# Decode attention over paged keys: both pages of a step in one score block, their rotary rows in one product and one transpose

## What is computed

```python
ckv_past = cache_ckv[page_table].reshape(b, past, KV_RANK)    # 16 pages of 128 positions x 256, per sequence
kr_past  = cache_krope[page_table].reshape(b, past, QK_ROPE)  # 128 positions x 64
sc = (einsum('bqhr,bkr->bhqk', q_lat, ckv) + einsum('bqhe,bke->bhqk', q_rope, k_rope)) * SOFTMAX_SCALE
p = softmax(sc); o_lat = einsum('bhqk,bkr->bqhr', p, ckv)
```

## Time and profile before

| | us |
|---|---|
| median of 3 runs | 518.49 |
| lowest, highest | 518.28, 519.22 |
| the profiled execution: its time | 518.8 |
| its span from first to last instruction | 517.0 |
| PE busy in the span | 501.8 |
| VectorE, ScalarE, GpSimd busy | 349.6, 287.0, 82.8 |

### The profile page before, as it was taken

The page is one execution under the profiler, slowest core; times in us unless marked ns, Lnnn a source line. Parts: engine busy times, 40 slices in busy tenths (PEclk is TensorE's granted clock), DMA queues, the critical chain, the costliest instruction groups (busy, mean ns, idle before and its releaser), DMA issues.

```text
span 517.0 us, 12185 instructions
## 1 busy us (share of the span) xinstructions
PE 501.8 (97%) x4738; PEld 443.0 (86%) x4738; DVE 349.6 (68%) x656; ACT 287.0 (56%) x588; POOL 82.8 (16%) x100
## 2 busy tenths in 40 slices
PE   8999999999999999999999999999999999999993
PEld 7999999899999999899999755666676699999992
DVE  4843668694657666653433468699987899997753
ACT  6543312206357275653624865689996879663631
POOL 1321000000001000000000142235554303100710
PEclk9999999999999999999999999999999999999997
DMA  8642112249798888979986152945625577879722
GB/s 260 242 163 83 63 61 103 88 133 344 242 316 301 285 298 278 335 255 312 295 299 215 46 136 39 232 120 118 153 74 210 203 248 217 287 238 334 258 90 82
DMA packets 58075, 104.15 MB, mean 201 GB/s; under 512 B 7465, under 2 KB 27346, under 8 KB 57890
## 3 DMA queue, kind: packets, MB, share of 16 engines
q1 hardware_dynamic: 58018, 103.37, 62.2%
HBM read 95.68 MB, written 7.76 MB: 200 GB/s over the span
## 4 chain that ended last, share of the span: by engine, by line
PE 81%; DVE 6%; ACT 5%; DMA 4%; issue 2%; POOL 0%; SPq 0%; DVEq 0%; ACTq 0%
PE pm L1632 17%; PE pm L1634 16%; PE pm L1633 16%; PE px L1728 4%; PE px L1748 3%; PE pm L1929 3%; PE pm L1859 3%; PE px L1910 2%; PE pm L1897 2%; DMA dec<-ac_dram 2%; DVE w_lo L992 2%; DMA w_raw<-in_w_out 1%; PE px L1850 1%; PE px L1873 1%; PE pm L1921 1%
## 5 line engine op out<-in xcount | busy, mean ns | idle before, releaser
L1632 PE MATMUL pm<-xw_hi,w_lo 128*128 128x260 f32 x544 | 158.0, 290 | 0.4 <-DVE xw_lo L1125 0.4
L1633 PE MATMUL pm<-xw_lo,w_hi 128*128 128x260 f32 x544 | 153.7, 283 | 0.0
L1634 PE MATMUL pm<-xw_hi,w_hi 128*128 128x260 f32 x544 | 153.6, 282 | 0.0
L595 ACT ACTIVATE w_hi<-w_raw 128x1024 fp32r<-128x1024 f32 (+1 forms) x70 | 72.6, 1038 | 85.5 <-PE pm L1634 70.1
L992 DVE TENSOR_TENSOR w_lo<-w_raw,w_hi 128x1024 fp32r<-128x1024 f32 (+1 forms) x70 | 84.8, 1219 | 32.1 <-ACT w_hi L595 32.1
L1632 PEld LDWEIGHTS pm<-xw_hi,w_lo 128*128 128x128 f32 x544 | 102.4, 188 | 2.9 <-issue 0.6
L1633 PEld LDWEIGHTS pm<-xw_lo,w_hi 128*128 128x128 f32 x544 | 102.5, 188 | 0.2
L1634 PEld LDWEIGHTS pm<-xw_hi,w_hi 128*128 128x128 f32 x544 | 102.4, 188 | 0.0
L1632 PE MATMUL pm<-mix_hi,w_lo 128*128 128x260 f32 x224 | 64.0, 286 | 1.6 <-DVE w_lo L992 1.4
L1634 PE MATMUL pm<-mix_hi,w_hi 128*128 128x260 f32 x224 | 63.4, 283 | 0.0
L1632 PEld LDWEIGHTS pm<-mix_hi,w_lo 128*128 128x128 f32 x224 | 42.2, 188 | 2.7 <-DVE w_lo L992 2.4
(11 more groups left out here) (289 smaller groups left out, 1076.6 us busy)
## 6 DMA issues: line engine op xcount, KB each, us to landing
page<-in_cache SPq DMA_DIRECT2D x128, 288.0 KB, 4.2
w_raw<-in_w_in SPq DMA_DIRECT2D x32, 512.0 KB, 5.2
w_raw<-in_w_out SPq DMA_DIRECT2D x32, 512.0 KB, 5.2
dec<-ac_dram SPq DMA_DIRECT2D x16, 256.0 KB, 9.5
hring<-in_ssm_state SPq DMA_DIRECT2D x8, 512.0 KB, 8.5
o_ssms<-hring SPq DMA_DIRECT2D x8, 512.0 KB, 6.6
w_raw<-in_w_qb SPq DMA_DIRECT2D x6, 384.0 KB, 2.8
xraw<-in_xT SPq DMA_DIRECT2D x8, 260.0 KB, 5.0
```

What stands on the lines that cost most here:

```text
L595: act.activation(w_hi[s][:, 0:n], w_raw[s][:, 0:n], ACT.Copy).then_inc(a_whi, 1)
L1632: pe.matmul(out, wl, xh, start=start, stop=False)
L1633: pe.matmul(out, wh, xl, start=False, stop=False)
L1634: return pe.matmul(out, wh, xh, start=False, stop=stop)
```

## The change

- Scores. The two pages of a step now share one block of 128 columns, `px[:, n%2, 0:128]`. The first page's heads stand in rows 0 to 7 of a sequence's 32, the second page's in rows 16 to 23 (`ROWS = 16`). `qlp` has 48 columns for each sequence with the heads in columns 16 to 23, and the window of 32 columns that starts at 16 or at 0 puts them in rows 0 to 7 or 16 to 23. The rotary rows of the two pages lie in the lower and the upper 64 partitions of one tile, so that one product of 128 columns (with `qr`, which has the lower query in columns 0 to 7 and the upper one in 16 to 23) serves both.
- Softmax. Each page's row group has its own maximum and sum; maximum, exponential and transpose take 128 columns in place of 256. ACT's copy of the transpose puts the two groups into the places that `values` reads (`ptb`, which GpSimd now sets to zero once). `values` has the products that it had.
- Joining. After steps 7 and 15 the two groups are joined: PE swaps the maxima and sums of the groups by a product with a permuted identity (`pair_swap`, `M_SWAP`), DVE takes the smaller of the negated maxima (`pair_max`), ACT computes two weights (`pair_weights`), DVE the common sum and the scaled output (`sample_out`), and adds the two groups after the transpose (`sample_out_t`). For the first four sequences these stand at item 31 (swap), item 32 (`sample_out`) and item 34 (`o_lat_t(0)`). For the others, swap at item 39; `o_lat_t(1)` and the C-B products move from ahead of the loop over n to n = 2 and n = 3.
- Loads. A page is 256 KB for a sequence; its rotary rows are in an array of their own and come in a further DMA of 32 KB to 64 partitions, so that SP issues 16 DMAs for a step in place of 8. The table is laid out so that one call reads four page numbers. `load_pair` reads the eight numbers, loads the first page, then the rotary rows of both pages (two buffers; those of step q wait for the scores of step q-2), then the second page.

The diff, without declarations of tiles and with the joining cut short:

```diff
-        def load_pages(n):
-            g, p, s = n // NPAGE, n % NPAGE, page_slot(n)
+        def indices(n):
+            return nc.values_load_multi_w_load_instructions(ptab[0:1, 4 * n:4 * n + 4], engines=[mybir.EngineType.SP])[1]
+        def load_page(n, index):
             if n >= NSLOT:
                 sp.wait_ge(p_pn, (n - NSLOT) // 2 + 1)
+            s = page_slot(n)
             for j in range(4):
-                at_ = (4 * g + j) * NPAGE + p
-                index = sp.value_load(ptab[0:1, at_:at_ + 1])
-                sp.dma_start(pages[s][:, j, :], a["cache"][bass.ds(index, 1)].rearrange("a p n -> p (a n)")).then_inc(s_pl[s], 16)
+                sp.dma_start(pages[s][:, j, :], a["cache"][bass.ds(index[j], 1)].rearrange("a p n -> p (a n)")).then_inc(s_pl[s], 16)
+        def load_pair(q_):
+            held = [indices(2 * q_ + half) for half in range(2)]
+            load_page(2 * q_, held[0])
+            if q_ >= 2:
+                sp.wait_ge(p_sc, q_ - 1)
+            for half in range(2):
+                for j in range(4):
+                    sp.dma_start(page_kr[q_ % 2][64 * half:64 * half + 64, j, :],
+                                 a["cache_kr"][bass.ds(held[half][j], 1)].rearrange("a p n -> p (a n)"))\
+                      .then_inc(s_pl[page_slot(2 * q_ + half)], 16)
+            load_page(2 * q_ + 1, held[1])
...
-            act.activation(ptb[:, n % 2, :], px[:, 2, 0:2 * P], ACT.Copy).then_inc(a_ptb, 1)
+            apart = ptb[:, n % 2, :].rearrange("p (x c) -> p x c", x=2)[:, :, 0:P].rearrange("p x (j m) -> p x j m", j=4)
+            act.activation(apart[:, :, :, 0:H], px[:, 2, 0:P].rearrange("p (j x m) -> p x j m", j=4, x=2)[:, :, :, 0:H], ACT.Copy)\
+               .then_inc(a_ptb, 1)
...
-            act.activation(psm[:, n % 2, :], px[:, n % 2, 0:2 * P], ACT.Exp, bias=nmh[:, g, p + 1:p + 2],
+            act.activation(psm[:, n % 2, :], px[:, n % 2, 0:P], ACT.Exp, bias=nmh[:, g, p + 1:p + 2],
...
-            link(dve.tensor_reduce(nmx[:, 0:1], px[:, n % 2, 0:2 * P], AX.X, ALU.max, negate=True))
+            link(dve.tensor_reduce(nmx[:, 0:1], px[:, n % 2, 0:P], AX.X, ALU.max, negate=True))
...
+        def sample_out(g):
+            dve.wait_ge(a_wt, 2 * g + 2)
+            link(dve.tensor_tensor(nmx[:, 6:7], nmh[:, g, HSTEP + 1:HSTEP + 2], nmx[:, 4:5], ALU.mult))
+            link(dve.scalar_tensor_tensor(nmx[:, 6:7], nmx[:, 2:3], nmx[:, 5:6], nmx[:, 6:7], ALU.mult, ALU.add))
+            link(dve.reciprocal(nmx[:, 7:8], nmx[:, 6:7]))
+            dve.wait_ge(v_upd, HSTEP * (g + 1))
+            dve.tensor_scalar(o_lat, ckbc[:, g, :], nmx[:, 4:5], nmx[:, 7:8], ALU.mult, ALU.mult).then_inc(v_ol, 1)
...
                 n_page = 2 * n + half
-                s = page_slot(n_page)
-                pe.wait_ge(s_pl[s], 64 * (n_page // NSLOT + 1))
-                for op in range(4):
+                s, c = page_slot(n_page), ROWS * (1 - half)
+                pe.wait_ge(s_pl[s], 128 * (n_page // NSLOT + 1))
+                for r in range(2):
                     for j in range(4):
-                        b = 4 * g + j
-                        w = (qlp[:, 0, b, :], qlp[:, 1, b, :], qrl[:, b, :], qru[:, b, :])[op]
-                        x = pages[s][:, j, (256, 384, 512, 512)[op]:(384, 512, 576, 576)[op]]
-                        lo_, n_ = P * half + (0, 0, 0, 64)[op], (128, 128, 64, 64)[op]
-                        last = pe.matmul(px[32 * j:32 * j + 32, n % 2, lo_:lo_ + n_], w, x, start=op == 0, stop=op == 3)
+                        pe.matmul(px[32 * j:32 * j + 32, n % 2, 0:P], qlp[:, r, 4 * g + j, c:c + 32],
+                                  pages[s][:, j, KVR + P * r:KVR + P * r + P], start=half == 0 and r == 0, stop=False)
+            for j in range(4):
+                last = pe.matmul(px[32 * j:32 * j + 32, n % 2, 0:P], qr[:, 4 * g + j, :], page_kr[n % 2][:, j, :],
+                                 start=False, stop=True)
             last.then_inc(p_sc, 1)
...
-            for half in range(2):
-                last = pe.transpose(px[:, 2, P * half:P * half + P], psm[:, n % 2, P * half:P * half + P], cm[:, M_ID, :])
-            last.then_inc(p_tr, 1)
+            pe.transpose(px[:, 2, 0:P], psm[:, n % 2, :], cm[:, M_ID, :]).then_inc(p_tr, 1)
...
+        def pair_swap(g):
+            pe.wait_ge(a_ptb, (HSTEP + 1, NSTEP - 1)[g])
+            if g:
+                pe.wait_ge(v_pair, 3)
+            else:
+                pe.wait_ge(v_upd, HSTEP)
+            pe.matmul(px[:, 2, KVR:KVR + 2], cm[:, M_SWAP, :], nmh[:, g, HSTEP:HSTEP + 2], start=True, stop=True).then_inc(p_pv, 1)
```

More of the change, by code:

```diff
@@ L235, in build @@
     o += 512
-    pages = [at(f"page{s}", [P, 4, 576], F, G_ + 9216 * s if s < 4 else o) for s in range(NSLOT)]
+    pages = [at(f"page{s}", [P, 4, 512], F, (G_, G_ + 8192, G_ + 16384, G_ + 28672, o)[s]) for s in range(NSLOT)]
+    page_kr = [at(f"page_kr{k}", [P, 4, PAGE], F, G_ + 24576 + 2048 * k) for k in range(2)]
     qs = [at(f"qs{h}", [P, NT], R, o + 2048 * k) for k, h in enumerate((2, 3, 4, 5))]
-    o += 9216
+    o += 8192
     qs = [at(f"qs{h}", [P, NT], R, o + 2048 * h) for h in range(2)] + qs
@@ L243, in build @@
     assert BASE + o <= nc.sbuf_usable_end, (BASE + o, nc.sbuf_usable_end)
-    cm, cols, rows, qlp, qrl, qru = (small[k] for k in ("cm", "cols", "rows", "qlp", "qrl", "qru"))
+    cm, cols, rows, qlp, qr = (small[k] for k in ("cm", "cols", "rows", "qlp", "qr"))
     ckbc, olT, xlast, dtt, acum, toend, ealast = (small[k] for k in ("ckbc", "olT", "xlast", "dtt", "acum", "toend", "ealast"))
-    nmh, alpha, rs, lsum, epsc, nmx, rsum = (small[k] for k in ("nmh", "alpha", "rs", "lsum", "epsc", "nmx", "rsum"))
+    nmh, alpha, rs, epsc, nmx, rsum = (small[k] for k in ("nmh", "alpha", "rs", "epsc", "nmx", "rsum"))
     ident_r = at("ident_r", [P, P], R, CM_ + 4 * P * M_MQ)
@@ L868, in _ @@
         act.preload_act_table_set("natural_log_exp_and_others")
+        pair_weights(1)
         for n in range(8):
@@ L1019, in evac @@
                     dve.tensor_scalar(q[:, 2 * it[1] + r // 2, halves[h]], src, SCALE, None, ALU.mult).then_inc(v_ev, 1)
+                for g in range(2):
+                    if (i, r) == (SWAPS[g][0], 0):
+                        if g:
+                            sample_l(NSTEP - 1).then_inc(v_pair, 1)
+                        pair_max(g)
         def dt_series(part):
@@ L1093, in sample_sum @@
                 dve.wait_ge(v_upd, n)
-            link(dve.scalar_tensor_tensor(own, own, alpha[:, n:n + 1], rs[:, n:n + 1], ALU.mult, ALU.add))
+            return dve.scalar_tensor_tensor(own, own, alpha[:, n:n + 1], rs[:, n:n + 1], ALU.mult, ALU.add)
+        def sample_sum(n):
+            g = n // HSTEP
+            if n < NSTEP - 1:
+                link(sample_l(n))
             dve.wait_ge(p_pn, n + 1)
@@ L1250, in _ @@
                 sample_conv()
+            if i == 32:
+                sample_out(0)
         sample_sum(NSTEP - 1)
@@ L1386, in _ @@
                 state(n - 1)
+            if n == 1:
+                sample_out(1)
             if n >= 5:
@@ L1665, in project @@
                         prob_t(turn[8 * r + k])
+                    for g in range(2):
+                        if (i, 8 * r + k) == SWAPS[g]:
+                            pair_swap(g)
                     if (i, 8 * r + k) == OSLOT:
-                        pe.wait_ge(a_ptb, HSTEP + 1)
+                        pe.wait_ge(a_ptb, HSTEP + 3)
                         o_lat_t(0)
@@ L1813, in extras @@
                     for r in range(2):
[L1814 to L1815 removed]
+                        pe.matmul(o_, qlp[:, r, b, ROWS:], ckv[:, r, NT + b:NT + b + 1], start=r == 0, stop=False)
+                    last = pe.matmul(o_, qr[:, b, :], kr[:, NT + b:NT + b + 1], start=False, stop=True)
                 last.then_inc(p_aux, 1)
@@ L1818, in _ @@
         for _ in range(6):
-            none = qlp[:, 0].rearrange("p b n -> p (b n)")
+            none = qlp[:, 0].rearrange("p b n -> p (b n)")[:, 0:256]
             pe.matmul(px[:, 3, 0:256], none[:, 0:P], none, start=True, stop=True)
@@ L1930, in outs, with cb_products @@
                       start=kb == 0, stop=kb == 3).then_inc(p_o, 1)
+        def cb_products():
+            pe.wait_ge(v_ol, 4)
+            for g in range(2):
+                for c in range(NCH):
+                    cs = slice(CH * c, CH * c + CH)
+                    last = pe.matmul(px[:, 2 + g, cs], xbc[:, 8 + g, cs], xbc[:, 10 + g, cs], start=True, stop=True)
+                last.then_inc(p_cb, 1)
         xs_t(0)
@@ L1934, in _ @@
         values_up(0)
-        o_lat_t(1)
         values_up(1)
-        pe.wait_ge(v_ol, 4)
-        for g in range(2):
-            for c in range(NCH):
-                cs = slice(CH * c, CH * c + CH)
-                last = pe.matmul(px[:, 2 + g, cs], xbc[:, 8 + g, cs], xbc[:, 10 + g, cs], start=True, stop=True)
-            last.then_inc(p_cb, 1)
         for n in range(2 * NCH):
@@ L1945, in _ @@
```

(5 more changed lines are left out.)

102 lines of the change are left out of this document (61 added, 41 removed).

## The result

The changed kernel takes 539.14 us (median of 4 runs, 538.79 to 540.37) where the kernel before takes 518.56 on the same chip (518.28 to 519.22). The ratio is 1.0392, 95% interval 1.0378 to 1.0406: 20.6 us slower, against a forecast of 514.2 with a range up to 520.5. The profiled execution took 538.79 us, its span 536.8.

What follows compares the result with a forecast made beforehand. PE was taken as the bound, busy 156.53 of 156.60 us; -3.5 -1.8 -0.2 +0.6 +0.1 +0.5 = -4.3 from the profiled 518.8 gave 514.5, so 514.2 us for the median, range 512.8 to 520.5.

Steps and rivals of the forecast that it cites:

- PE's part: PE's work in the score steps: rotary products save 0.22 us a step (3.5 in all), one transpose 0.115 (1.8 in all).
- 0.3 us wait ahead of the latent transpose: PE's wait for ACT's copy before the first latent output's transpose: predicted to go, taken as 0.2 us saved.
- (c): Rival on rotary products: cost goes by instruction, not column, saving 0.33 in place of 0.22 us a step; 512.4 us; chance 0.03.
- (d): Rival on joining: swaps wait 0.5 us each, the order behind the stage costs 1.0; 516.2 us; chance 0.10 together with some late pages.
- (b): Rival on DMA engines: at share 0.87 they may have no more to give; time stays at 518 to 519; chance 0.07.
- SP's 9.2 us: SP's queue: predicted issue work per step after the change, said to fit within PE's step of 10.1 us.
- the margin: SP's queue: predicted room per step between its issue work and PE's step of 10.1 us, 0.9 us.
- price of a DMA to 64 partitions: SP's issue of one rotary DMA: taken as 0.333 us from the page load's row, bounds 0.25 to 0.58.
- rival (a): SP's queue becomes the bound once issue work passes 10.1 us a step; net 16 times the excess less 4.7; chance 0.20.
- The sign to tell (a) from (b): PE waits for pages in most steps: SP without idle time means (a); with idle time and longer landing, (b).
- The read of four numbers: SP's read of four page numbers in one call: taken as 0.4 us, bounds 0.27 to 1.2.
- Late pages: PE's waits for page loads in the score steps: some steps come close to a wait, 0.5 us in all, bounds 0 and 3.

Runs made afterwards that it cites:

- GpSimd run: The changed kernel, computing the same, with all eight rotary DMAs of a step issued by GpSimd in place of SP: 514.57 us, ratio 0.9905.
- folded run: The changed kernel with rotary rows back in the 288 KB page load and their products as before the change; one score block, one transpose, joining kept: 517.02 us.
- run with two rotary DMAs a step: The changed kernel, but from step 2 each half's rotary rows come in one 128 KB DMA from fixed places, not four by page number: 516.34 us.
- run at 0.333 us an issue: The changed kernel, but each rotary DMA puts its 32 KB into 128 partitions of 256 bytes in place of 64 of 512: 522.55 us.
- 16 B run: The changed kernel, but from step 2 each rotary DMA moves only 16 bytes to each of its 64 partitions: 539.1 us, ratio 1.0371.

## Why the prediction was wrong

**PE's part was right.** In the GpSimd run an undisturbed step takes 9.94 us, before 10.28: 0.34, where the sum had 0.22 + 0.115 = 0.335. The folded run splits it: 0.12 from the transpose, so 0.22 from the rotary products. Timeline, PE, the GpSimd run, one transpose and one swap between products of the projection, against the earlier trace rows:

```profile
192.43 0.29 PE L1712 MATMUL pm<-xw_hi,w_hi 128*128 128x260 f32 x1
192.55 0.27 PE L1823 MATMUL px<-cm,psm 128*128 128x128 f32 x1
...
192.78 0.28 PE L1711 MATMUL pm<-xw_lo,w_hi 128*128 128x260 f32 x1
...
220.53 0.28 PE L1712 MATMUL pm<-xw_hi,w_hi 128*128 128x260 f32 x1
220.65 0.28 PE L1842 MATMUL px<-nmh,cm 128*128 128x2 f32 x2
...
221.00 0.28 PE L1711 MATMUL pm<-xw_lo,w_hi 128*128 128x260 f32 x1
```

From the product ahead (L1712) to L1711 stand, beside the transpose or the swap, two projection products, 0.24 us. The transpose costs 0.35 - 0.24 = 0.11 us, the swap 0.47 - 0.24 = 0.23 (I had 0.3, and it waits for nobody), the 0.3 us wait ahead of the latent transpose is gone, and behind the last score, where the earlier trace rows stand, the span is 0.5 us shorter than before (234.4 against 234.9), some 0.3 of it the rest of step 15. Rivals (c) and (d) did not occur. The rule for (b), the share of 0.87 as a ceiling, fell too: the GpSimd run has 0.88 with 296 GB/s, nearly the 302 that I said the change would want, and the run with two rotary DMAs a step 0.92 with 304.

**The step that failed is SP's 9.2 us.** By terms, for a step:

| | predicted | measured, changed kernel |
|---|---|---|
| eight page DMAs | 8 x 0.505 = 4.0 | 8 x 0.515 = 4.1 |
| eight rotary DMAs | 8 x 0.505 = 4.0 | 8 x 0.651 = 5.2 |
| reads of two times four numbers, weights | 0.6 + 0.5 | 0.66 + 0.5 |
| long issues | none | about 0.6 |
| idle, and what is left | none | about 0.6 |
| sum | 9.2 | 11.64 |

(0.515 and 0.651 are medians from start to start. The long issues are the 14 over 0.7 us in the stage, together 9.2 us above 0.45 each, over 15 steps. The 9.2 of the prediction has 0.30 for a read; with the 0.4 that its text takes it would have been 9.4, and the margin 0.7 us in place of 0.9.)

The first mis-sized term is the price of a DMA to 64 partitions. I had two rows with 64 partitions, 0.525 and 0.58 (the least of its row, whose median is 0.613), and one page load with 128, 0.333, and took the last because source and address were of the same kind. What mattered was the form, 64 partitions or 128; the measured 0.469 lies by the rows that I set aside, and above the 0.45 that the rival (a) names as the point from which it decides. It is worth 1.2 us a step.

The second is what I left out: long issues. They stood in the rows before, as the maximum of L397, 1.195 us. There they cost nothing, since SP had 3 us of idle time in a step; a queue near its bound pays each of them. The run at 0.333 us an issue shows this term apart: by its terms 8 x 0.515 + 4.1 + 0.66 + 0.5 = 9.4, measured some 10.4 of work in steps of 10.58, and seven waits of PE. So even if the DMA had had the price that I gave it, 16 issues a step would have ended the gain. With 0.651 and no long issue the sum is 10.5; with them 11.1; the last 0.5 is idle time of SP (3.0 us in 15 steps, 0.20) and issues slightly above their median.

The formula of rival (a), 16 times the excess over 10.1 us less 4.7, gives with 11.64 us 24.6 - 4.7 = +19.9; measured were +20.6. Since the step is the measured one, this tests the arithmetic and not the price. The mechanism of rival (a) and its arithmetic were right; the sizes of its single cases were too small, and I had given it a chance of only 0.20. The sign to tell (a) from (b), SP's idle time, did so.

**The read of four numbers** takes 0.298 us, little more than a read of one (0.269), where I took 0.4 and the rule in "Runtime: NRT & Kernel Launch" of the Trainium skill, section on instruction fetch mechanics, would have it near 0.85 for each. The page tells of loads from HBM; for a read from SBUF the trace disagrees with it.

**Late pages.** The margins that I worked out (2.3 us more of issue, late by at most 1 us in some steps) assumed that SP caught up at each wait for a page buffer. With 11.4 us of work in a step of 11.64 it never catches up. (The bound for step 0 was also added up wrong: 124.7 and 2.3 are 127.0, not 126.5, and so past the 125.49 at which the page is used.)

## What to carry to other kernels

A queue that issues DMAs is an engine: add up its starts, not its durations, over the period of the loop, with its own maxima in the sum, and compare with the bound's period. By medians alone, 9.4 us of issue in a period of 9.94 failed here and 7.9 us (twelve DMAs) held: the long issues need the room between. When a change splits a load, price the new DMA by a row with the same destination partitions; if it doesn't fit, give it to the queue of an engine that has nothing due soon, here GpSimd, which kept the whole gain, and not to ScalarE, which is busy about half of the time but owes a result in every step.

## What the hardware showed that I had not expected

- The issue of a DMA on SP takes 0.469 us to 64 partitions, with 512 B or 16 B in each, 0.333 to 128, 0.316 to 32; ScalarE's queue has 0.492 and GpSimd's 0.518 for the 64-partition form. From start to start on SP the 64-partition form costs 0.65 us, and 0.64 where the address is constant, in which case the instruction itself shows 0.597.
- One read of four numbers from SBUF into registers costs 0.298 us, one of one 0.269.
- About once a step an issue takes 0.8 to 1.8 us. In the changed kernel 12 of the 14 issues over 0.7 us overlap a 16 KB DMA of the instruction kind, 14 of 15 in the 16 B run, 14 of 15 in the run to 128 partitions. That is no matter of chance: of all 257 issues of the changed kernel's stage only 27 overlap one, and it has 15 such DMAs. The stretch around one of them (DMA queues: packets, MB, share of 16 engines), in which L412 has its 1.79 us:

```profile
q1 hardware_dynamic: 294, 0.67, 87.9%
q8 instruction: 1, 0.02, 4.6%
```

  Whether one causes the other was not tried, and stays open.
- Beside two long waits the granted clock fell. It is 0.98 over the stage of the changed kernel because it stands at 0.50 (the 1.2 GHz level) in two stretches of 3.41 us, and at 1.00 (2.4 GHz) in the rest. They stand by PE's two longest waits of the stage: the first begins 0.7 us behind one of 2.35 us (the row below), the second 0.5 us before the end of one of 2.56 us. The timeline row, then the windows of both stretches:

```profile
185.42 0.65 PE L1788 MATMUL px<-page,qlp 128*32 128x128 f32 x16 [2.35 <-DMA page<-in_cache]
```

```profile
186.17:189.58 3.41, 3.41 (x20) 3.37 (x16) 1.71 (x6) 1.92 (x5) 0.19 (x1) 0.50 0.98 374
210.06:213.48 3.42, 2.94 (x31) 2.50 (x32) 1.07 (x4) 0.64 (x3) 0.00 (x0) 0.50 0.87 304
```

  In the first stretch the projection products start 0.22 us apart in place of 0.12, and the two steps are the longest of all, 14.4 and 14.0 us. The 4342 products are busy for 501.6 us in the changed kernel and 496.5 in the GpSimd run, whose stage has no such stretch. By these rows little of it adds to the 20.6 us, though no run tests that: SP sets the pace, and in the whole stage it waits longer than 0.4 us only once, 0.93 us at 216.9, behind the second stretch.
